# The first norm's modulation in four groups of two chunks, woven into the first pair of weight products

## The reference

```
def modulation(cond, w_mod, b_mod):
    m = jax.nn.silu(cond) @ w_mod + b_mod        # 1024 x 9216 per layer
    return jnp.split(m, N_MOD, axis=-1)          # shift, scale, gate, three times
def rmsnorm(x, w):
    y = xf * lax.rsqrt(jnp.mean(xf * xf, axis=-1, keepdims=True) + EPS)
    return (y * w.astype(jnp.float32)).astype(x.dtype)
def modulate(x, w, shift, scale):
    return rmsnorm(x, w) * (1 + scale) + shift
x = x + 0.5 * g1 * swiglu(modulate(x, nw[0], sh1, sc1), ffn1_up[l], ffn1_down[l])
ctx = ctx + 0.5 * cg1 * swiglu(modulate(ctx, nw[0], ch1, cs1), ffn1_up[l], ffn1_down[l])
```

## Time and profile before

| | |
|---|---|
| median of 3 runs | 3000.36 us (2999.95 to 3000.66) |
| the profiled execution | 2998.74 us, its span 2997.0 us |
| TensorE matmul, weight load busy | 2949.3 us (98%), 2515.6 us (84%) |
| VectorE, ScalarE, POOL busy | 1563.6 us (52%), 830.4 us (28%), 262.6 us (9%) |
| DMA | 273.65 MB, 91 GB/s over the span |

### The profile page before, as it was taken

How to read it: one execution, slowest core, us unless ns; L and a number is a source line. 1 busy time by engine, 2 the same in 40 slices (tenths; PEclk the granted TensorE clock), 3 DMA queues, 4 the chain that set the end, 5 groups by cost and what they waited for, 6 DMA issues and landing times.

```text
span 2997.0 us, 41788 instructions
## 1 busy us (share of the span) xinstructions
PE 2949.3 (98%) x16404; PEld 2515.6 (84%) x16404; DVE 1563.6 (52%) x2570; ACT 830.4 (28%) x1142; POOL 262.6 (9%) x260
## 2 busy tenths in 40 slices
PE   7999999999999999999999999999999999999998
PEld 5888888888888888888888888888888788888886
DVE  6676777557343348767775762222236644433333
ACT  4211211243332233212112421111235343432223
POOL 2000000022600020000000200000011500200001
PEclk8999999999999999999999999999999999999999
DMA  6444434222012224444432432222113123333331
GB/s 216 120 120 131 123 113 136 68 66 50 26 50 62 70 63 142 132 121 127 126 114 83 119 94 62 64 63 63 58 43 78 47 67 94 92 98 94 96 95 65
DMA packets 455618, 273.65 MB, mean 91 GB/s; under 512 B 9754, under 2 KB 453828, under 8 KB 455492
## 3 DMA queue, kind: packets, MB, share of 16 engines
q1 hardware_dynamic: 453348, 267.90, 31.3%
q10 hardware_dynamic: 2144, 4.00, 0.4%
HBM read 269.77 MB, written 2.10 MB: 91 GB/s over the span
## 4 chain that ended last, share of the span: by engine, by line
PE 93%; DVE 3%; ACT 2%; issue 1%; DMA 0%; SPq 0%; POOL 0%; DVEq 0%; ACTq 0%; POOLq 0%
PE ps L1260 55%; PE ps L1267 28%; PE ps L1435 2%; PE ps L1283 2%; PE ps L1440 1%; PE ps L714 1%; PE ps L694 1%; DVE first_acc L1769 1%; PE ps L1317 1%; PE ps L683 1%; ACT hhi L1600 0%; DMA first_mod<-in_w_mod 0%; DVE hlo L1825 0%; PE ps L596 0%; DVE x L1976 0%
## 5 line engine op out<-in xcount | busy, mean ns | idle before, releaser
L1260 PE MATMUL ps<-hhi,whi 128*128 128x512 f32 x3136 | 889.1, 351 | 0.5 <-ACT whi L1529 0.5
L1260 PE MATMUL ps<-hlo,whi 128*128 128x512 f32 x3136 | 879.9, 348 | 0.0
L1702 DVE TENSOR_TENSOR wlo<-wraw,whi 128x1024 fp32r<-128x1024 f32 x371 | 457.0, 1232 | 596.5 <-ACT whi L1529 593.4
L1529 ACT ACTIVATE whi<-wraw 128x1024 fp32r<-128x1024 f32 x371 | 391.4, 1056 | 921.7 <-PE ps L1267 888.7
L1267 PE MATMUL ps<-hhi,wlo 128*128 128x512 f32 x3136 | 627.7, 349 | 0.0
L1260 PEld LDWEIGHTS ps<-hhi,whi 128*128 128x128 f32 x3136 | 500.4, 188 | 85.5 <-issue 6.2
L1267 PEld LDWEIGHTS ps<-hhi,wlo 128*128 128x128 f32 x3136 | 499.6, 188 | 82.2 <-issue 3.2
L1260 PEld LDWEIGHTS ps<-hlo,whi 128*128 128x128 f32 x3136 | 500.4, 188 | 79.6 <-issue 0.5
L1716 DVE SCALAR_TENSOR_TENSOR macc<-modraw,cond,macc 128x256 f32<-128x256 f32 x896 | 366.4, 480 | 0.1
L1260 PE MATMUL ps<-mhi,whi 128*128 128x512 f32 (+1 forms) x1184 | 334.2, 349 | 4.1 <-DVE mlo L1966 2.9
L1260 PE MATMUL ps<-mlo,whi 128*128 128x512 f32 (+1 forms) x1184 | 332.7, 348 | 0.0
(11 more groups left out here) (193 smaller groups left out, 2301.1 us busy)
## 6 DMA issues: line engine op xcount, KB each, us to landing
wraw<-in_ffn_up SPq DMA_DIRECT2D x176, 512.0 KB, 3.9
modraw<-in_w_mod SPq DMA_DIRECT2D x66, 1024.0 KB, 5.2
wraw<-in_ffn_down SPq DMA_DIRECT2D x64, 512.0 KB, 4.1
wraw<-in_w_in SPq DMA_DIRECT2D x64, 512.0 KB, 4.0
wraw<-in_ffn_down SPq DMA_DIRECT2D x32, 384.0 KB, 3.3
wraw<-in_w_out SPq DMA_DIRECT2D x16, 512.0 KB, 4.0
first_mod<-in_w_mod SPq DMA_DIRECT2D x6, 1024.0 KB, 12.2
wraw<-in_w_br_pool SPq DMA_DIRECT2D x16, 256.0 KB, 2.7
```

The costliest lines, as they stand in the source:

```text
L1260: nc.tensor.matmul(o, whi[:, slot, k, :], a[:, k * NT + t0:k * NT + t0 + n], start=(k == 0 and a is hi), stop=False)
L1529: nc.scalar.activation(whi[:, slot2], wraw[:, slot4], ACT.Copy).then_inc(hi_split, 1)
L1702: nc.vector.tensor_tensor(wlo[:, slot2], wraw[:, slot4], whi[:, slot2].bitcast(F32), ALU.subtract).then_inc(lo_split, 1)
```

## The change

The prologue is by four groups. Group g has the shift and scale columns of chunks 2g and 2g+1 (jobs g and g+4). All eight jobs are done on TensorE: `condp` holds the two condition columns padded with zeros to 32, `first_products(g)` writes chunk k's product in strip k mod 4 of the bank, ScalarE copies the whole bank (`first_copy`), and `first_sums` folds the strips and turns the rows in one product with `fold`. VectorE's `first_modulation(g)` adds biases and makes the amplitudes of two chunks. The order of the first norm's chunks becomes two latent, two context, by group (`chunk_at`, `place_of`). In `first_pair` the next group's products stand between the two latent chunks of a group and its sums in front of the context chunks. The last latent and context chunks of the last group are followed by a tail by unit of two chunks.

The token blocks are loaded by one DMA each, transposed block by block, copied by VectorE (`copy_x`), and squared from the rows by ScalarE with an accumulated sum (`row_squares`), so that POOL and TensorE have no part in the first norm's sum of squares. Units 0 and 1 are loaded between groups 0 and 1.

```diff
+            for g in range(GROUPS):
+                for part in range(2):
+                    j = g + GROUPS * part
+                    sp.dma_start(first_mod_columns(g, part), wm[0][:, :, j * 2 * P:(j + 1) * 2 * P]
+                                 ).then_inc(first_loaded[j], 16)
+                if g == 0:
+                    for s in range(2):
+                        load_unit(s, s, ...)
...
+                def steps_of():
+                    if a == 0:
+                        for g in range(GROUPS):
+                            for n_pt in range(2):
+                                ks = (2 * g, 2 * g + 1)
+                                if (g, n_pt) == (GROUPS - 1, 1):
+                                    yield from ((n_pt, k, (s,)) for s in range(2) for k in ks)
+                                else:
+                                    yield from ((n_pt, k, (0, 1)) for k in ks)
+                        return
...
+            for b in range(NBLK):
+                pe.wait_ge(s_x[b], 16)
+                at_least(pe, xt_used, b - 1)
+                for j in range(DC):
+                    mm = nc.tensor.transpose(bank(2 * (b % 2), j * P, P), xrow[:, b, j * P:(j + 1) * P], ident[:])
                 mm.then_inc(xt_ready, 1)
+                if b == 2:
+                    pe.wait_ge(s_rows, 16 * 15)
...
+            def first_products(g):
+                for part in range(2):
+                    pe.wait_ge(first_loaded[g + GROUPS * part], 16)
+                    columns = first_mod_columns(g, part)
+                    out = first_mod_ps(g)[:, 2 * P * part:2 * P * (part + 1)]
+                    for k in range(DC):
+                        q = k % (P // BLK)
+                        mm = nc.tensor.matmul(out[BLK * q:BLK * (q + 1)], condp[:, k, :], columns[:, k, :],
+                                              start=(k < P // BLK), stop=(k >= DC - P // BLK), skip_group_check=True)
+                mm.then_inc(first_made, 1)
+            def first_sums(g):
+                pe.wait_ge(first_row, g + 1)
+                for b in range(4):
+                    mm = nc.tensor.matmul(bank(5, 8 * g + 2 * b, 2), mod_row[:, g % 2, b * P:(b + 1) * P], fold[:, 0:2],
+                                          start=True, stop=True)
+                mm.then_inc(mod_sum, START_JOBS // GROUPS)
+            def first_inside(n_pt, k):
+                g, odd = divmod(k, 2)
+                if g + 1 < GROUPS:
+                    if odd and not n_pt:
+                        first_products(g + 1)
+                    if not odd and n_pt:
+                        first_sums(g + 1)
+            pe.wait_ge(cond_ready, 1)
+            first_products(0)
             pe.wait_ge(rec_ready, 1)
...
+            first_sums(0)
+            pe.wait_ge(xt_used, NBLK)
...
+            def first_copy(g):
+                act.wait_ge(first_made, g + 1)
+                nc.scalar.activation(mod_row[:, g % 2, :], first_mod_ps(g), ACT.Copy).then_inc(first_row, 1)
...
+            first_copy(0)
             split_hi(0, 0, 0)
             split_hi(*second_unit(plan[0]))
+            for i in range(2 * DC):
                 hi_chunk(i, 0, 0, 0, BOTH, h_row)
+                if i % 4 == 1 and i // 4 + 1 < GROUPS:
+                    first_copy(i // 4 + 1)
...
+            reciprocals(0, BOTH)
+            split_lo(0, 0, 0)
             dve.wait_ge(bc_ready, 1)
+            dve.wait_ge(xt_used, NBLK)
+            for g in range(GROUPS):
+                first_modulation(g)
+                for i in range(4 * g, 4 * g + 4):
+                    norm_step(i, 0, 0, 0, BOTH, h_row, ps[:, 3072:3072 + NT])
+                    if i == 0:
+                        split_lo(*second_unit(plan[0]))
...
-            clear_squares(0)
-            for j in range(SQ_ADDED):
-                add_squares(j, BOTH, j + 1, j + 1)
             odd_chunks(0, BOTH)
```

More of the change, by code:

```diff
@@ L347, in build @@
     s_mask = sem("s_mask")
-    s_x = [sem(f"x_landed{i}") for i in range(2)]
+    s_x = [sem(f"x_landed{i}") for i in range(NBLK)]
     s_rows = sem("s_rows")
@@ L448, in at_least, with first_mod_columns, first_mod_ps, chunk_at @@
             eng.wait_ge(s, value)
[L450 to L458, removed]
+    def first_mod_columns(g, part):
+        return first_mod[:, g - 1, part] if g else first_mod0[:, part]
+    def first_mod_ps(g):
+        return bank(4 - g % 2)
+    def chunk_at(a, i):
+        return (i // 2 % 2, 2 * (i // 4) + i % 2) if a == 0 else divmod(i, DC)
+    def place_of(a, part, k):
+        return 4 * (k // 2) + 2 * part + k % 2 if a == 0 else part * DC + k
     class Steps:
@@ L1275, in first_pair, with products @@
                 halves = parts is LATENT_HALVES
+                def steps_of():
[8 more added lines that the diff above has]
+                        return
+                    for n_pt, (t0, _) in enumerate(parts):
+                        tail = DC if n_pt < len(parts) - 1 else DC - (2 if t0 == 0 else 4)
+                        yield from ((n_pt, k, (0, 1)) for k in range(tail))
+                        yield from ((n_pt, k, (s,)) for s in range(2) for k in range(tail, DC))
                 pe.wait_ge(lo_split, unit + 2)
-                for n_pt, (t0, n) in enumerate(parts):
-                    def products(k, s, terms):
+                for n_pt, k, units in steps_of():
+                    t0, n = parts[n_pt]
+                    def products(s, terms):
                         o = pair_ps(buf, s, LATENT[0])[:, t0:t0 + n] if halves else pair_ps(buf, s, (t0, n))
@@ L1287, in products @@
                         return mm
[L1289 to L1305, removed]
+                    i = place_of(a, n_pt, k)
+                    if units[0] == 0:
+                        inside(n_pt, k)
+                    pe.wait_ge(hhi_ready, h_base(a) + i + 1)
+                    for s in units:
+                        products(s, ((whi, hhi), (wlo, hhi)))
+                    pe.wait_ge(*h_part(a, i))
+                    for s in units:
+                        mm = products(s, ((whi, hlo),))
+                        if n_pt == len(parts) - 1 and k == DC - 1:
+                            mm.then_inc(w_used, 1)
             def norm_sum(parts, used, squares):
@@ L1358, in _ @@
-            pe.wait_ge(set_up, 1)
[L1360 to L1392, removed]
+            for b in range(NBLK):
[3 more added lines that the diff above has]
+                    mm = nc.tensor.transpose(bank(2 * (b % 2), j * P, P), xrow[:, b, j * P:(j + 1) * P], ident[:])
+                mm.then_inc(xt_ready, 1)
+                if b == 2:
+                    pe.wait_ge(s_rows, 16 * 15)
+                    for l in range(DEPTH):
+                        mm = nc.tensor.transpose(bank(7, l * P, ROWS[l]), vrow[0:ROWS[l], l, :],
+                                                 ident[0:ROWS[l], 0:ROWS[l]])
+                    mm.then_inc(vec_t, 1)
@@ L1396, in _ @@
             mm.then_inc(bc_ready, 1)
[L1397 to L1403, removed]
+            first_sums(0)
+            pe.wait_ge(xt_used, NBLK)
             def second_half(n_ph):
+                if n_ph == 0:
+                    return first_inside
                 def inside(n_pt, k):
                     before = plan[n_ph - 1]
-                    if n_ph and before["ahead"]:
+                    if before["ahead"]:
                         if (n_pt, k) == (0, 2):
@@ L1579, in tail @@
                     norm_chunk(ph, i)
[L1581 to L1586, removed]
             def root(n, parts):
@@ L1610, in _ @@
             act.dma_start(ident[:], t["const_ident"]).then_inc(s_ident, 16)
-            act.dma_start(xrow[:, 0:XBLK, :], t["x"][0].rearrange("(b p) n -> p b n", p=P)).then_inc(s_x[0], 16)
-            act.dma_start(xrow[:, XBLK:NBLK, :], t["ctx"][0].rearrange("(b p) n -> p b n", p=P)).then_inc(s_x[1], 16)
+            for b in range(NBLK):
+                rows = t["x"][0, b * P:(b + 1) * P] if b < XBLK else t["ctx"][0, (b - XBLK) * P:(b - XBLK + 1) * P]
+                act.dma_start(xrow[:, b, :], rows).then_inc(s_x[b], 16)
@@ L1618, in _ @@
             ins.then_inc(cond_ready, 1)
[L1619 to L1623, removed]
-            act.wait_ge(set_up, 1)
-            root(0, BOTH)
+            for b in range(XBLK, NBLK):
+                row_squares(b)
+            act.wait_ge(set_up, 1)
+            act.wait_ge(row_squared, NBLK - 1)
@@ L1751, in reciprocals @@
                 nc.vector.reciprocal(tok[:, b:b + nb], tok[:, b:b + nb]).then_inc(rec_ready, 1)
[L1753 to L1760, removed]
-                        reciprocals(0, BOTH)
-                    for c in range(2):
-                        acc = first_acc[:, 2 * i:2 * i + 2, c, :]
-                        scalar = cond[:, c * DC + k:c * DC + k + 1]
-                        if k == 0:
-                            ins = nc.vector.tensor_scalar(acc, columns[:, :, 0, :], scalar, None, ALU.mult)
-                        else:
```

(22 more changed lines are left out.)

96 lines of the change are left out of this document (39 added, 57 removed).

## The result

The changed kernel takes 2981.61 us (median of 4 runs, 2980.53 to 2982.88) against 3000.15 before (2999.78 to 3000.66): ratio 0.9938, 95% interval 0.9926 to 0.995, 18.5 us less. The forecast was 2990 with a range of 2982 to 2996. The sign is right, the time is 0.4 us under the range, and the gain is 18.5 where 10.3 was worked out. The profiled execution took 2981.54, span 2979.3.

What follows compares the result with a forecast made beforehand. TensorE's chain bounds it, so the second pair's start counts: 75.94 - 65.1 - 0.5 = 10.3 us gained; from 2998.74 that gives 2988.4, and the median 1.6 above, 2990 us; range 2982 to 2996.

Steps and rivals of the forecast that it cites:

- What bounds the kernel: TensorE's chain, 93%; a prologue change is worth what it moves the first pair's end at 75.94, plus lateness right behind.
- 65.1 + 0.5: First pair's products end at 65.1 us, then a new 0.5 us stall for the whi split of unit 2.
- P: Length of one group's 32 strip instructions in first_products at full clock: taken as 3.7 us, ends 1.8 and 7.1.
- The rows of 0.59 and 1.02: Earlier profile's two-strip state products: 8 instructions took 0.59 us and 16 took 1.02, used to judge strip overlap.
- free overlap: Two-strip state products with strips fully side by side: would give 0.49 and 0.92 us.
- the in-order picture: A product's second instruction waits for its first, beside the next product's first; more than two strips bring nothing: 3.7 us.
- The start: First weight product of the first pair at 29.6 us instead of 57.12.
- 3.7 + 1.2 = 4.9: Group 0's strip products from 19.1 us: 3.7 at full clock plus 1.2 for a cold clock, ending at 24.0.
- Period of a group: Groups 1 and 2 of the first pair: latent products, strip products, sums, context products and a wait, 9.5 us each.
- The waits: New TensorE waits: 0.7 us for hhi three times, 0.5 for POOL's hlo in group 3, 0.5 for unit 2's whi.
- Full overlap: First rival: four strips run side by side, strip products 1.8 us instead of 3.7, 7.6 more gained, 2983; chance 0.25.
- A cold pair: Rival: TensorE, broken up by waits, stays at 1.2 GHz through the first pair, 15 us slower, 3015; chance 0.04.

Runs made afterwards that it cites:

- the three kernels: Changed kernel with its 32 strip instructions in two strips (2987.44 us), in one strip (3000.77 us), or in four strips with neighbouring products sharing one (2978.77 us).
- the kernel with earlier sums: Changed kernel with, from the second group on, the next group's products ahead of both latent chunks and its sums between them: 2976.54 us.
- the second execution of the change: The profiled execution when the changed kernel was run again, unaltered, on another chip; that run's median was 2979.79 us.

## Why the prediction was off

- **What bounds the kernel, and that only the second pair's start counts: right.** 18.1 of the 18.5 us are that shift. The second pair came at 57.80 where the prediction has 65.1 + 0.5, 7.8 us earlier; the four bursts make 7.3 of it, the rest of the start 2.3, and 1.8 went the other way.
- **The strips: the step that failed.** The prediction took "the second waits for the first, and the next product's first runs beside it", and P = 3.7. Measured: 1.86, which was its lower end and its first rival (0.25). Its error is one of reading. The rows of 0.59 and 1.02 were held against free overlap with a constant of 0.06 (0.43 + 0.06 and 0.85 + 0.06, which the prediction writes as 0.49 and 0.92) and against the in-order picture with 0.06 + 0.107. Both have the same slope with two strips and differ in the constant alone, and a constant of 0.16 explains them as well: 0.43 + 0.16, 0.85 + 0.16. Rows of two strips could not tell the pictures apart. By the number of strips they differ at once, as the three kernels show. This cost 2 x 1.84 for groups 2 and 3 and 1.8 for group 1 (3.07 with its cold part against 4.9), and another 1.8 at the start.
- **The start: the other miss, 4.1 us (25.5 against 29.6).** The term "3.7 + 1.2 = 4.9" behind 19.1 was 1.07 behind 18.87. Of the 3.8, 1.8 are P; 0.8 that half of the products ran at the first landing, which the prediction had not split though the code waits part by part; and 1.2 the clock, which had not fallen in this execution (it had in the second). The remaining 0.2 is the landing. So part of this gain is luck of the execution. From those products on, the chain took 5.6, as worked out.
- **Period of a group: 8.15 against 9.5.** The products account for -1.84; the latent products beside the strips took 0.5 more (1.66 and 1.60 for six, against 1.375 each). Of that, 0.1 belongs to the first product behind the wait (36.12 to 36.46, 0.34 where the next take 0.23). Full-width products away from strips and sums kept their pace (six in 1.38 in the kernel with earlier sums, 49.64 to 51.02), so I put the other 0.4 down to the changes to strips and sums and back, argued, not tried by itself; the prediction had bounded it at 1.4 for all. The rule of the Trainium skill that it weighed (TensorEngine Tiling (Array Packing), Key Properties: a change of mode drains TensorE) fits: about 0.4 a group, three times 1.2, with the 0.16 of each burst besides.
- **The waits: right in place and size**, 0.73, 0.57 and 0.50 as shown above. No DMA released a product of groups 1 to 3, as forecast.
- **The rivals.** Full overlap was put at 2983 and is what happened; with the start's 2 us beside P it gives 2981. The Trainium skill's figure for four row strips (TensorE: Matmul & The Clock Gate, Measured speedup vs the span model: 3.07 times) would have P at 2.3; this form measured 7.02/1.86 = 3.8 times. A cold pair did not come: the clock was full from about 31 us on.
- **The range** was cut at 2982 on the argument that full overlap gives 2983 "with a microsecond to spare". By its own sum full overlap is 2990 - 7.6 = 2982.4, so only 0.4 was to spare, and the start's own uncertainty (half a group early, clock not fallen: 2 us) was not added to that end.

## What to carry to other kernels

Before a model is fitted to a few rows, ask whether the rival model, with a free constant, fits them too; if only the constant differs, the rows decide nothing and the range keeps both ends whole. fp32 products with 32-column results went four at a time when their results lay in four 32-partition strips (1.86 us against 7.02 in one). The small products woven between big ones ran at full clock (1.86); ahead of them, waiting for data, they cost twice (3.61). When a new wait stands at a round's start, move its producer one piece earlier: here that gave about 3.4 us on top of the change, read from traces.

## What the runs showed of the hardware that I had not expected

The time from the second pair on is the same program in all these kernels, yet it took 2918.0 to 2922.3 us in all the other profiled executions of the changed kernel and its variants, and 2927.7 in that of the kernel with earlier sums (2984.61 us, while its median is 2976.54). What differs is the granted clock in the middle of the layers; in that execution (columns as above):

```profile
800.00:805.00 5.00, 5.00 (x38) 4.68 (x36) 1.23 (x1) 2.87 (x4) 2.01 (x1) 0.95 0.29 65
805.00:810.00 5.00, 5.00 (x18) 4.32 (x18) 0.30 (x1) 0.28 (x1) 0.00 (x0) 0.50 0.13 40
810.00:815.00 5.00, 5.00 (x26) 4.35 (x26) 0.00 (x0) 1.01 (x1) 0.00 (x0) 0.87 0.00 0
```

PE was busy throughout and still ran at 1.2 GHz from just before 805 to after 810. Ahead of the dip stood two runs of twelve products with one moving column (L727, from 801.63 and 803.67). The second execution of the change has the same two runs (from 805.05 and 807.10) and a clock of 1.00 there, so they alone do not bring it. In stretches of 100 us up to 2900 this execution shows a clock of 0.97 or 0.98 in five behind the first pair, the second execution of the change in none. Whether such a dip comes differs from one execution of the same kernel to the next. So differences of 2 to 4 us are read from traces at a fixed place in the program, not from a few medians.
